# Products that nobody reads, in TensorE's waits amid the heads of both attentions of a two-layer decoder trunk

## The reference, cut to what matters

```
lg = einsum(q, k) * scale            # 256 x 256, causal, so 128 x 128 and 128 x 256
lg = lg + bias (layer 0) ; lg = where(allowed, lg, -inf)
p  = softmax(lg)
o  = einsum(p, v)
```

## Time and profile before

| | us |
|---|---|
| median of 3 runs | 1298.28 |
| lowest and highest | 1296.72, 1298.48 |
| the profiled execution's own time | 1298.05 |
| its span | 1296.2 |
| PE busy | 1243.5 (96%) |
| DVE busy | 339.2 (26%) |
| ACT busy | 286.8 (22%) |
| mean granted TensorE clock | 0.992 |

### The profile page before, as it was taken

One profiled execution on the slowest core, in us unless ns is written; L12 is line 12 of the kernel. 1 busy time (PEld: TensorE's weight loads), 2 busy tenths in 40 slices (PEclk: granted clock), 3 DMA queues, 4 the chain that ended last, 5 costly groups with the idle time before them and its releaser, 6 DMA issues.

```text
span 1296.2 us, 27225 instructions
## 1 busy us (share of the span) xinstructions
PE 1243.5 (96%) x12500; PEld 718.2 (55%) x12501; DVE 339.2 (26%) x701; ACT 286.8 (22%) x499; POOL 39.3 (3%) x48
## 2 busy tenths in 40 slices
PE   7998999999999999999999999999998999998896
PEld 6865788888756774344653344663342664333364
DVE  5877565445347550010010020010010000001001
ACT  5575562425237621010000000000000000000000
POOL 1012000000002200000000000000000000000000
PEclk9999999999998999999999999999999999999999
DMA  9632455365353389999999999999999999999994
GB/s 351 229 130 81 147 188 181 118 228 165 88 192 122 145 361 419 409 418 426 424 425 425 425 426 426 425 424 425 426 426 426 425 425 423 427 425 425 427 422 172
DMA packets 64108, 423.64 MB, mean 327 GB/s; under 512 B 5760, under 2 KB 13686, under 8 KB 39414
## 3 DMA queue, kind: packets, MB, share of 16 engines
q1 hardware_dynamic: 62780, 419.09, 80.0%
q0 software_dynamic: 992, 2.69, 0.7%
q10 hardware_dynamic: 218, 0.08, 0.0%
HBM read 420.77 MB, written 1.07 MB: 325 GB/s over the span
## 4 chain that ended last, share of the span: by engine, by line
PE 82%; DMA 10%; DVE 4%; ACT 3%; issue 1%; SPq 0%; DVEq 0%; ACTq 0%
PE PS L2305 33%; PE PS L2334 16%; PE PS L1733 7%; PE PS L1734 7%; PE PS L1737 7%; DMA places_raw<-in_w_down_o_dram 6%; DMA places<-in_w_down_o_dram 3%; PE PS L2068 2%; PE PS L2342 2%; PE PS L2244 1%; DVE w_r L947 1%; PE PS L2227 1%; PE PS L1857 1%; ACT w_r L487 1%; PE PS L2080 1%
## 5 line engine op out<-in xcount | busy, mean ns | idle before, releaser
L2305 PE MATMUL PS<-places_raw,xe 128*32 128x512 f32 (+1 forms) x3760 | 362.3, 540 | 10.2 <-DMA places_raw<-in_w_up_o_dram 10.1
L2305 PEld LDWEIGHTS PS<-places_raw,xe 128*32 128x32 f32 x3760 | 119.4, 110 | 240.1 <-issue 219.3
L1733 PE MATMUL PS<-w_r,a_hi 128*128 128x512 f32 (+4 forms) x400 | 148.2, 374 | 5.3 <-DVE a_lo L976 4.4
L1734 PE MATMUL PS<-w_r,a_lo 128*128 128x512 f32 (+4 forms) x400 | 145.6, 368 | 0.0
L947 DVE TENSOR_TENSOR w_r<-raw,w_r 128x2048 fp32r<-128x2048 f32 (+4 forms) x61 | 128.9, 2144 | 44.0 <-ACT w_r L487 43.9
L2305 PE MATMUL PS<-places,xe 128*32 128x512 f32 (+1 forms) x1360 | 133.3, 540 | 4.0 <-DMA places<-in_w_up_o_dram 4.0
L487 ACT ACTIVATE w_r<-raw 128x2048 fp32r<-128x2048 f32 (+4 forms) x61 | 106.5, 1801 | 14.9 <-PE PS L1737 13.1
L2334 PE MATMUL PS<-places_raw,e_l 128*32 128x256 f32 x1848 | 106.4, 380 | 2.1 <-DMA places_raw<-in_w_down_o_dram 2.1
L1737 PE MATMUL PS<-w_r,a_hi 128*128 128x512 f32 (+4 forms) x400 | 103.2, 365 | 0.3 <-DVE w_r L947 0.3
L2305 PEld LDWEIGHTS PS<-places,xe 128*32 128x32 f32 x1360 | 43.2, 110 | 87.8 <-issue 80.3
L1733 PEld LDWEIGHTS PS<-w_r,a_hi 128*128 128x128 f32 x400 | 76.3, 191 | 19.6 <-issue 7.0
(11 more groups left out here) (328 smaller groups left out, 1029.4 us busy)
## 6 DMA issues: line engine op xcount, KB each, us to landing
places_raw<-in_w_gate_o_dram SPq DMA_DIRECT2D x48, 1792.0 KB, 26.5
places_raw<-in_w_up_o_dram SPq DMA_DIRECT2D x46, 1792.0 KB, 31.1
places_raw<-in_w_down_o_dram SPq DMA_DIRECT2D x44, 1792.0 KB, 37.0
places<-in_w_down_o_dram SPq DMA_DIRECT2D x19, 1792.0 KB, 36.3
places<-in_w_up_o_dram SPq DMA_DIRECT2D x18, 1792.0 KB, 31.6
places<-in_w_gate_o_dram SPq DMA_DIRECT2D x16, 1792.0 KB, 30.2
raw<-in_w_in_e_dram SPq DMA_DIRECT2D x12, 1024.0 KB, 10.3
raw<-in_w_down_e_dram SPq DMA_DIRECT2D x11, 1024.0 KB, 5.0
```

The costliest lines, as they stand in the source:

```text
L1733: nc.tensor.matmul(dst, xh, wh, start=first, stop=False)
L1734: nc.tensor.matmul(dst, xl, wh, start=False, stop=False)
L2305: ins = nc.tensor.matmul(PS[g * Q:(g + 1) * Q, bank + c0 // NT, 0:c], xe[:, at, x0:x0 + Q], w[:, g * QW + c0:g * QW + c0 + c], start=at == ...
```

## The change

A table `BUSY` gives a number of products for some heads. A new helper `keep_busy(bank, times)` issues that many products of the identity with itself, float32, 128 x 128, into a PSUM bank that nothing reads before it is written again. In layer 0 they stand in front of the turns of heads 0, 1, 9, 11 and 13, each behind a wait on `tile_read` that makes the bank safe to write (bank 0 after tile 4's read, bank 2 after tile 5's). In layer 1 they stand in front of the logits of head 18 (3 products, behind a wait on `item_read`), and in front of the turns of heads 16 (5) and 17 (2), with no wait of their own.

```diff
+BUSY = {0: 4, 1: 4, 9: 4, 11: 7, 13: 4, NH: 3, NH + 1: 5, NH + 2: 2}

+            def keep_busy(bank, times):
+
+                for _ in range(times):
+                    nc.tensor.matmul(PS[:, bank, 0:P], ident, ident, start=True, stop=True)
+
             def head_turn(h):
 
+                if h < 2:
+                    pe.wait_ge(sem("tile_read"), 5)
+                    keep_busy(0, BUSY[h])
+                elif h in BUSY:
+                    pe.wait_ge(sem("tile_read"), 6 if h < 10 else 7)
+                    keep_busy(2, BUSY[h])
                 pe.wait_ge(sem("at_norm0"), h + 1)
                 pe.wait_ge(sem("at_norm"), h + 1)
...
                     if s < n:
                         h = h0 + s
+                        if s == 2:
+                            pe.wait_ge(sem("item_read"), 2 * GROUPS - 1)
+                            keep_busy(0, BUSY[NH])
                         pe.wait_ge(sem("grp_ev"), 2 * (s + 1))
...
                     if 3 <= s <= n + 2:
                         h = h0 + s - 3
+                        if s < 5:
+                            keep_busy(0, BUSY[NH + s - 2])
                         pe.wait_ge(sem("at_norm0"), h + 1)
```

## The result

The changed kernel takes 1301.10 us (median of 20 runs, 1298.66 to 1304.08) against 1296.79 us for the kernel before (20 runs beside it, 1294.43 to 1300.13). The ratio is 1.0028 with a 95% interval of 1.0019 to 1.0036: slower by some 3.6 us by the ratio and 4.3 by the medians. The forecast was 1298.5. The time is 2.6 us above it, and inside the range (1295.8 to 1301.2) by 0.1. That it lies inside is luck in part: the sum started from 1298.05, which is 1.3 us above the median of the kernel before beside it. Counted as a difference, the forecast was +0.4 and the range's upper end +3.1, and the medians differ by 4.3. The likeliest case was "no change that can be told", within 2.6 us; by ratio and medians the change is slower than that (the interval's lower end is 2.5 us).

What follows compares the result with a forecast made beforehand. The prediction took PE to bound the kernel, with 82% of the chain, then memory streaming from about 460 us. Terms +2.7 + 0 - 2.3 = +0.4 on 1298.05 gave 1298.5 us, range 1295.8 to 1301.2.

Steps and rivals of the forecast that it cites:

- The likeliest case: Whole kernel: no change that can be told, under 2.6 us (0.2%) either way; chance 0.73.
- Heads 0 and 1: Before turns 0 and 1: the wait on tile 4's read loses the clock and delays tile 5's squares, +2.7 us.
- 1.80 did not hold the clock: Before 81.04 us: PE's 1.80 us of work lost the clock before, so 1.1 us now would too; +2.7, not +1.0.
- The price of a product: All places: one product takes 0.22 us at full clock, taken from L1835; ends 0.11 and 0.43.
- Heads 9, 11 and 13: Before turns 9, 11 and 13: PE gains clock but turn 13 still waits for ACT, 0 us.
- second rival: Output projection after turn 13: the lost clock moves there and costs +1.7 us, total 1300.2; chance 0.13.
- Layer 1: Around 405 us: clock kept, so the 4.87 us behind turn 17 take half; -2.3 us.
- The sum: Whole kernel: +2.7 + 0 - 2.3 = +0.4 us on 1298.05, giving 1298.5.
- Span 1296.2 and 1.85 around it: Base of the sum: the profiled execution's 1298.05 us, made of its span and the time outside it.
- third rival: Products hold the clock nowhere: +2.7 at heads 0 and 1, +1.4 in layer 1, total 1302.2; chance 0.10.
- first rival: Heads 0 and 1: the clock is kept there too, +1.0 - 2.3 = -1.3 us, total 1296.8; chance 0.27.

Runs made afterwards that it cites:

- e3: Kernel before plus only layer 1's products (3, 5, 2), against the kernel before: ratio 0.9983, span -2.05 us.
- e4: Kernel before plus only the products before turns 9, 11 and 13 (4, 7, 4), against the kernel before: ratio 0.9999, span +0.20 us.
- e9: Kernel before plus 33 products that TensorE jumps over, against the kernel before: ratio 1.0015, 3.93 us outside the span.
- e11: The kernel before run again unchanged, for a second trace, beside the kernel before: ratio 0.9994.
- e1: Kernel before plus only the wait and products at heads 0 and 1, against the kernel before: ratio 1.0033, span +3.50 us.
- e2: Kernel before plus only the wait for the fifth tile_read before turns 0 and 1, no products, against the kernel before: ratio 1.0012, span +2.05 us.
- e5: The full changed kernel again, on another chip, against the kernel before: ratio 1.0033, span +2.75 us, 3.92 us outside it.
- e10: 18 products (heads 0, 1 in bank 7 without wait; layer 1) plus 10 before layer 0's down projection, against the kernel before: ratio 0.9988.
- e6: Only the products of heads 0 and 1, in bank 7 without the new wait, against the kernel before: ratio 1.0000, span -0.35 us.
- e7: Changed kernel, all 33 products, heads 0 and 1 in bank 7 without their wait, against the kernel before: ratio 0.9995, span -3.35 us.
- e8: 18 products: heads 0 and 1 in bank 7 without the wait, and layer 1, against the kernel before: ratio 0.9984, span -2.80 us.

## Why the prediction was right or wrong

**Heads 0 and 1, forecast +2.7.** The mechanism was right in each step: the wait on tile 4's read, the idle of 2.6 us (2.59), the clock lost behind it, turn 1 late (8.48 us after the group's start, before 4.39, so 4.1 as forecast), ACT's second copy, its split and the squares as what is late next, and the delay passed on whole to turn 13. Against the trace of before the term is +2.47. What failed is the base: the sentence "1.80 did not hold the clock". Five traces have the old code at this place, and in four of them (e3, e4, e9, e11) the clock did hold; the squares then came 10.56 to 10.58 us after the group's start, and not 12.03. All four traces with the wait (the changed kernel, e1, e2, e5) lost the clock. So the usual price is 14.50 - 10.57 = 3.9 us, less the share of executions in which the kernel before paid 1.5 of them itself; measured 3.50. One execution had been taken for the kernel. The price of a product was low too: 0.22 us was taken, and it was 0.25 at full clock and 0.45 at half.

**Heads 9, 11 and 13, forecast 0.** Right: +0.20 in e4's span, which can't be told from 0. The 7 products took turn 11's wait whole, the clock held from there on, and turn 13 gave it back to ACT, as worked out. The second rival, a fall behind turn 13, exists and costs 1.5 us (e11, e10), near its 1.7. But it is no child of the change: the kernel before shows it (e11). Its condition does not hold as stated either, since in e6 the clock held behind an idle of 2.84 us.

**Layer 1, forecast -2.3.** Right: -2.26 between the traces and -2.05 in e3's spans. The order was right too, with turn 17 bound by POOL's row and half of the stretch behind it won.

**The sum, forecast +0.4.** The spans say +2.05 by their medians (1297.25 against 1295.20 from another session; +2.75 in e5). The parts by themselves give 3.50 + 0.20 - 2.05 = +1.65. Of the 1.25 us between the parts' sum and the forecast, 0.8 were mis-sized at heads 0 and 1; the other terms are 0.20 and 0.25 off. The 0.4 us between 1.65 and 2.05 are within the scatter of the runs.

**Outside the span, not forecast at all.** "Span 1296.2 and 1.85 around it" took the 1.85 as fixed. With all 33 products it is 3.8 to 4.0, whether they run (changed kernel, e5, e7) or not (e9), and with 28 or fewer it is 1.8. That is 1.9 to 2.1 of the 4.3 us, about half of the slowdown, and it turned a case within the bound of 0.2% into one beyond it. It also brought the time next to the third rival's 1302.2, though of that rival only the wait at heads 0 and 1 happened and its +1.4 in layer 1 did not. Which property of TensorE's program matters between 28 and 33 products stays open: its length, or where parts of it come to lie. So does where in the execution the 2 us pass, since the trace shows only the span.

The first rival's clock kept at heads 0 and 1 happens only without the wait: in four of four traces with the products (e6, e7, e8, e10) and in four of five with neither. The Trainium skill's rule on transposes (TensorE: Matmul & The Clock Gate, Part 4), which spoke for it, did not decide: eight products that count by it were there in the changed kernel, and the clock fell. It fell with the wait in all four traces, with products (the changed kernel, e1, e5) or without (e2). No run here tests whether transposes count. The third rival falls: in layer 1 the clock held in six of six traces with the products, and in one of seven without.

## What to carry to other kernels

Products that are to keep the clock up belong into the idle that is there. If their target needs a new wait, choose another target (bank 7 here), or the filler makes a longer hole than the one it should fill: the wait alone cost 2.05 us here, and without it the same products cost nothing. They pay only where TensorE is the chain behind the hole and where the clock falls in most executions; of three places one paid, 2.1 us.

A fall of the clock in one trace is one draw. Look at a second trace of the same kernel before you price it, and give the time outside the span a term of its own. A fall that comes and goes was worth 1.5 us here, as much as most of the effects in question.

## What the runs showed of the hardware that was not expected

- Instructions that are never executed cost time outside the span: 1.82 us with the program as it was, 3.93 with 33 float32 products more in a part that TensorE jumps over (e9). With 28 more, executed, it was 1.84 (e10), and with 15 and 18 no more (e4, e8): it did not grow with the number up to there.
- With the same code at a place, the clock behind its wait falls in some executions and not in others: behind turns 0 and 1 in one of five traces, behind turn 11 in six of nine. Behind the wait of 2.6 us it fell in four of four, once for 6.7 us (e5); behind 2.44 us at 279 us in eight of twelve; behind 2.83 to 2.84 us before turn 13 in two of three (e10, e11, and not e6).
- A product of 128 x 128 times 128 columns in float32 takes 0.25 us at full clock, four in a row behind a wait (81.53 - 80.54 for four), and 0.45 at half (85.36 - 83.56); 0.22 and 0.43 were taken from L1835.
